# Heads of a gated mixer: one masked step in place of three decay levels, the first turned inverse copied by ScalarE, another order on VectorE

## What is computed

```python
def hgrn2_chunked(q, k, v, log_f):
    b_cum = jnp.cumsum(log_f, axis=3)
    def step(S, inp):
        q_c, k_c, v_c, b_c = inp
        inter = jnp.einsum('bhtk,bhkv->bhtv', q_c * jnp.exp(b_c), S)
        diff = b_c[:, :, :, None, :] - b_c[:, :, None, :, :]
        decay = jnp.exp(jnp.where(causal, diff, -jnp.inf))
        scores = jnp.einsum('bhtk,bhsk,bhtsk->bhts', q_c, k_c, decay)
...
def gated_delta_chunked(q, k, v, beta, g):
...
    A = jnp.where(strict, jnp.einsum('bhntk,bhnsk->bhnts', kb, k) * Lmat, 0.0)
    T = lax.linalg.triangular_solve(eye + A, jnp.broadcast_to(eye, A.shape),
                                    left_side=True, lower=True, unit_diagonal=True)
```

## Time and profile before

| | |
|---|---|
| median of 3 runs | 1363.9 us (1363.88 to 1363.91) |
| the profiled execution, its own time | 1364.0 us |
| its span, first to last instruction | 1362.3 us |
| TensorE busy | 1348.9 us, 99% |
| VectorE busy | 1044.2 us, 77% |
| ScalarE busy | 797.6 us, 59% |
| DMA, mean over the span | 167 GB/s, 227.80 MB |
| granted TensorE clock | 1.000 of 2.4 GHz |

### The profile page before, as it was taken

The page is one execution under the profiler, slowest core; times in us unless marked ns, Lnnn a source line. Parts: engine busy times, 40 slices in busy tenths (PEclk is TensorE's granted clock), DMA queues, the critical chain, the costliest instruction groups (busy, mean ns, idle before and its releaser), DMA issues.

```text
span 1362.3 us, 24396 instructions
## 1 busy us (share of the span) xinstructions
PE 1348.9 (99%) x8590; PEld 1210.5 (89%) x8590; DVE 1044.2 (77%) x1644; ACT 797.6 (59%) x1352; POOL 29.4 (2%) x72
## 2 busy tenths in 40 slices
PE   8999999999999999999999999999999999999998
PEld 8888888989888888888899999999999998988887
DVE  5798888777666686666778898898898877666665
ACT  4445554644334364444668898898898853544444
POOL 6000000000000010000000000000000000000000
PEclk9999999999999999999999999999999999999999
DMA  8565555556555756666564444554543286666661
GB/s 267 153 194 153 149 147 160 190 194 206 185 185 187 226 150 209 186 185 185 155 183 136 132 123 131 135 148 115 149 131 123 88 211 203 173 205 197 191 186 62
DMA packets 291214, 227.80 MB, mean 167 GB/s; under 512 B 10882, under 2 KB 270164, under 8 KB 291156
## 3 DMA queue, kind: packets, MB, share of 16 engines
q1 hardware_dynamic: 291012, 226.75, 56.0%
q10 hardware_dynamic: 144, 0.26, 0.1%
HBM read 225.90 MB, written 1.08 MB: 167 GB/s over the span
## 4 chain that ended last, share of the span: by engine, by line
PE 93%; DVE 3%; ACT 1%; issue 1%; DVEq 1%; ACTq 0%; DMA 0%; POOL 0%; SPq 0%; POOLq 0%
PE M L2119 10%; PE G L2119 9%; PE M L2107 7%; PE M L2108 7%; PE M L2109 7%; PE G L2102 5%; PE G L2104 5%; PE G L2103 5%; PE M L2121 5%; PE G L2121 5%; PE G L2245 2%; PE G L3007 2%; PE M L2830 1%; PE M L2812 1%; PE G L3009 1%; PE G L2109 1%
## 5 line engine op out<-in xcount | busy, mean ns | idle before, releaser
L1241 DVE TENSOR_TENSOR w_lo<-w_raw,w_hi 128x2048 fp32r<-128x2048 f32 (+2 forms) x247 | 478.0, 1941 | 126.4 <-ACT w_hi L655 120.6
L655 ACT ACTIVATE w_hi<-w_raw 128x2048 fp32r<-128x2048 f32 x197 | 375.9, 1909 | 169.5 <-PE M L2121 54.3
L2102 PE MATMUL G<-xa,w_hi 128*128 128x256 f32 x592 | 176.9, 299 | 0.0
L2104 PE MATMUL G<-xa,w_lo 128*128 128x256 f32 x592 | 167.3, 283 | 0.0
L2103 PE MATMUL G<-xa,w_hi 128*128 128x256 f32 x592 | 167.0, 282 | 0.0
L2119 PE MATMUL M<-xa,w_hi 128*128 128x512 f32 x600 | 151.6, 394 | 0.0
L2119 PE MATMUL G<-xa,w_hi 128*128 128x512 f32 x568 | 142.4, 393 | 0.0
L2119 PEld LDWEIGHTS M<-xa,w_hi 128*128 128x128 f32 x600 | 107.8, 189 | 19.8
L2119 PEld LDWEIGHTS G<-xa,w_hi 128*128 128x128 f32 x568 | 104.0, 188 | 21.2 <-issue 1.2
L2107 PE MATMUL M<-w_hi,xb 128*128 128x512 f32 x300 | 117.3, 391 | 0.1
L2108 PE MATMUL M<-w_lo,xb 128*128 128x512 f32 x300 | 117.1, 390 | 0.0
(11 more groups left out here) (461 smaller groups left out, 2545.2 us busy)
## 6 DMA issues: line engine op xcount, KB each, us to landing
w_raw<-in_w_in SPq DMA_DIRECT2D x150, 512.0 KB, 4.7
w_raw<-in_ffn_w_in SPq DMA_DIRECT2D x88, 512.0 KB, 5.0
w_raw<-in_w_ff SPq DMA_DIRECT2D x64, 512.0 KB, 4.1
w_raw<-in_ffn_w_out SPq DMA_DIRECT2D x44, 512.0 KB, 4.9
w_raw<-in_w_in SPq DMA_DIRECT2D x33, 256.0 KB, 3.2
w_raw<-in_w_out SPq DMA_DIRECT2D x16, 512.0 KB, 4.1
w_raw<-in_w_branch_gdn SPq DMA_DIRECT2D x16, 512.0 KB, 5.3
w_raw<-in_w_branch SPq DMA_DIRECT2D x12, 512.0 KB, 4.2
```

Source lines behind the costliest of these rows:

```text
L655: nc.scalar.activation(w_hi[:, slot, :], w_raw[:, slot, :], ACT.Copy).then_inc(hi_ready, 1)
L1241: return v.tensor_tensor(dst, src, hi.bitcast(F32), ALU.subtract)
L2102: mm(out_, w[0], x[0], start=first, stop=False)
L2104: return mm(out_, w[1], x[0], start=False, stop=last_)
```

## The change

Levels 0, 1 and 2 become one step, still called level 0, for groups of four tokens. middle(0) subtracts from hb the value at the second token of each group, and caps the last one's distance from below at -80 (FAR). level_exp(0) makes both exp(-d) and exp(d) for all 256 columns. decayed(0) makes decayed keys and decayed queries in full. level(0) multiplies them in two 128 x 128 matmuls (the second block with its operands exchanged), at the place of level(1). VectorE clears sct with a memset, settles, and scored(0) copies under a group mask. GpSimd builds the two group masks into the free slots lmask 1 and lmask_t 0, with four additions. The counts of the semaphores follow (7 steps a head in place of 8 or 9; step_of).

inv_t(0) and y_copy(0) go: ScalarE writes yc from yi with four copies of 64 partitions, at the end of the head before, ahead of z_copy(1). n21's copy moves to behind level_exp(3). On VectorE inverse(1) comes ahead of both halves of w_low for chunk 1 and scored(0) behind them. In head(0), middle(0) and w_low for the next head's chunk 0 come ahead of the copy of tok. In the loop, middle(0) stands where middle(1) and middle(2) stood.

The diff, cut to its core:

```diff
@@ -624,6 +633,12 @@
 
         for l in range(LEVELS):
             level(l)
+        settle()
+        done(nc.gpsimd.tensor_tensor(lmask[:, 1, :], lmask[:, 1, :], lmask[:, 0, :], ALU.add))
+        done(nc.gpsimd.tensor_tensor(lmask_t[:, 0, :], lmask_t[:, 0, :], lmask_t[:, 1, :], ALU.add))
+        settle()
+        done(nc.gpsimd.tensor_tensor(lmask[:, 1, :], lmask[:, 1, :], ident[:], ALU.add))
+        done(nc.gpsimd.tensor_tensor(lmask_t[:, 0, :], lmask_t[:, 0, :], ident[:], ALU.add))
 
         c = FIRST["ffn1"]
         slot = c % RING
...
@@ -969,8 +984,12 @@
                 ins.then_inc(tap_ready, 1)
 
             def level_exp(l, turn=i):
-                act.wait_ge(dd_ready, l + (turn - 1) * 8)
+                act.wait_ge(dd_ready, step_of(l) + 1 + (turn - 1) * STEPS_H)
                 buf = dd[:, l % 2, :]
+                if l == 0:
+                    nc.scalar.activation(dd[:, 1, :], dd[:, 0, :], ACT.Exp, scale=-1.0)
+                    nc.scalar.activation(dd[:, 0, :], dd[:, 0, :], ACT.Exp).then_inc(lev_exp, 1)
+                    return
                 if l == 8:
                     nc.scalar.activation(buf[:, 0:P], buf[:, 0:P], ACT.Exp, scale=-1.0)
                     nc.scalar.activation(buf[:, P:T], hb[:, P:T], ACT.Exp).then_inc(lev_exp, 1)
@@ -1009,10 +1028,8 @@
             def y_copy(l):
                 if not main:
                     return
-                act.wait_ge(yt_done, l + 1 + (i - 1) * 6)
-                if l == 0:
-                    nc.scalar.activation(yc.rearrange("p i c -> p (i c)"), M[:, 5, 0:T], ACT.Copy).then_inc(yy_ready, 1)
-                elif l < LEVELS - 2:
+                act.wait_ge(yt_done, l + (i - 1) * 5)
+                if l < LEVELS - 2:
                     nc.scalar.activation(halved(yc.rearrange("p i c -> p (i c)"), l, 1), halved(M[:, 5, 0:T], l, 1),
                                          ACT.Copy).then_inc(yy_ready, 1)
                 else:
@@ -1074,7 +1091,6 @@
                 o_hi(1, 0, 2)
             if main:
                 z_copy(1)
-                y_copy(0)
             if not gemm:
                 o_hi(2, 2, 4)
             if main:
@@ -1087,6 +1103,7 @@
                 z_copy(2)
                 y_copy(1)
                 level_exp(3)
+                nc.scalar.activation(n21, nt[:, :, :, HD:P], ACT.Copy)
             if not gemm:
                 split_half(FIRST["yh"] + 2, 0)
             compact(2)
...
@@ -1194,9 +1211,12 @@
                 for side in range(2):
                     ins = nc.scalar.activation(kept(xc, side), quad(x0, side), ACT.Copy)
                 ins.then_inc(xc_ready, 1)
-                level_exp(1, i + 1)
-                level_exp(2, i + 1)
-                nc.scalar.activation(n21, nt[:, :, :, HD:P], ACT.Copy)
+                level_exp(0, i + 1)
+                for side in range(2):
+                    half = slice(HD * side, HD * side + HD)
+                    for e in range(2):
+                        ins = nc.scalar.activation(yc[HD * e:HD * e + HD, :, half], yi[half, :, e, half], ACT.Copy)
+                ins.then_inc(yy_ready, 1)
 
         head(0, True, False)
         with act.Fori(1, GH) as i:
@@ -1787,6 +1807,13 @@
             def middle(l):
                 if l > 2 and not main:
                     return
+                if l == 0:
+                    fours = hb.rearrange("p (n s) -> p n s", s=4)
+                    far = dd[:, 0, :].rearrange("p (n s) -> p n s", s=4)
+                    v.tensor_tensor(far, fours, fours[:, :, 1:2].to_broadcast([P, T // 4, 4]), ALU.subtract)
+                    settle()
+                    v.tensor_scalar(far[:, :, 3:4], far[:, :, 3:4], -FAR, None, ALU.max).then_inc(dd_ready, 1)
+                    return
                 if l == 8:
                     v.tensor_tensor(dd[:, 0, 0:P], hb[:, 0:P], hb[:, P - 1:P].to_broadcast([P, P]), ALU.subtract
                                     ).then_inc(dd_ready, 1)
@@ -1799,7 +1826,11 @@
             def decayed(l):
                 if not main:
                     return
-                dve.wait_ge(lev_exp, l + (i - 1) * 8)
+                dve.wait_ge(lev_exp, step_of(l) + 1 + (i - 1) * STEPS_H)
+                if l == 0:
+                    v.tensor_tensor(kqd[:, 0, :], hk, dd[:, 1, :], ALU.mult)
+                    v.tensor_tensor(kqd[:, 1, :], hq, dd[:, 0, :], ALU.mult).then_inc(wl_ready, 1)
+                    return
                 sz = 1 << (l - 1)
                 if l == 8:
                     v.tensor_tensor(kqd[:, 0, 0:P], hk[:, 0:P], dd[:, 0, 0:P], ALU.mult)
@@ -1813,12 +1844,12 @@
             def scored(l):
                 if not main:
                     return
-                dve.wait_ge(lev_done, l + 1 + (i - 1) * 9)
+                dve.wait_ge(lev_done, step_of(l) + 1 + (i - 1) * STEPS_H)
                 ps = M[:, 2 - 2 * (l % 2), 0:P] if 0 < l < 8 else M[:, 1 if l == 0 else 2 if gemm else 0, 0:T]
-                both_b = [P, 2, P]
                 if l == 0:
-                    v.tensor_tensor(sct[:, 0:T].rearrange("p (i c) -> p i c", i=2), ps.rearrange("p (i c) -> p i c", i=2),
-                                    ident[:].unsqueeze(1).to_broadcast(both_b), ALU.mult).then_inc(sc_used, 1)
+                    dve.sem_inc(waited, 1)
+                    v.copy_predicated(sct[:, 0:T].rearrange("p (i c) -> p i c", i=2), group_masks.bitcast(I32),
+                                      ps.rearrange("p (i c) -> p i c", i=2)).then_inc(sc_used, 1)
                 elif l == 8:
                     v.tensor_copy(sct[:, P:3 * P], ps).then_inc(sc_used, 1)
                 else:
@@ -1871,24 +1902,25 @@
 
             if not gemm:
                 o_low(1, 0, 2)
-            decayed(1)
-            decayed(2)
-            if main and gemm:
-                w_low_half(c0 + 4 + RING - 6, 0, i, 6)
+            decayed(0)
             inverse(1)
+            if main:
+                v.memset(sct[:, 0:T], 0.0)
             if not gemm:
                 o_low(2, 2, 4)
             if main and gemm:
+                w_low_half(c0 + 4 + RING - 6, 0, i, 6)
                 w_low_half(c0 + 4 + RING - 6, 1, i, 6)
+            if main:
+                settle()
             scored(0)
             middle(3)
-            scored(1)
             if main and gemm:
                 w_low_half(c0 + 5 + RING - 6, 0, i, 6)
             inverse(2)
             middle(4)
             decayed(3)
-            scored(2)
+            settle()
             middle(5)
             decayed(4)
             inverse(3)
@@ -2015,8 +2047,8 @@
                 v.scalar_tensor_tensor(out=hk, in0=eh, scalar=lb1[:, ds(i, 1)], in1=hr,
                                        op0=ALU.mult, op1=ALU.mult).then_inc(qk_ready, 1)
                 settle()
-                middle(1)
-                middle(2)
+                if main:
+                    middle(0)
                 v.tensor_tensor(mt, kk[:, 1, :].unsqueeze(1).to_broadcast([P, 2, P]), lt[:, :, P:T], ALU.mult)
                 settle()
                 dve.wait_ge(qk_done, i + 1)
@@ -2024,12 +2056,13 @@
                     ins = v.scalar_tensor_tensor(out=lt[:, e, :], in0=M[:, 3, 0:3 * P], scalar=QSCALE, in1=lt[:, e, :],
                                                  op0=ALU.mult, op1=ALU.mult)
                 ins.then_inc(lt2_ready, 1)
+                if not main:
+                    middle(0)
+                    w_low(c0 + 3 + RING, i, 6)
                 dve.wait_ge(tok_done, i + 1)
                 v.tensor_copy(tok[:, 0, :], G[:, 1, :]).then_inc(evac[1], 1)
                 if main:
                     delta_out_low(i)
-                else:
-                    w_low(c0 + 3 + RING, i, 6)
             settle()
 
         dve.sem_inc(ogl_ready, 1)
...
@@ -2769,15 +2802,11 @@
             def level(l):
                 if not main:
                     return
-                if l == 0:
-                    pe.wait_ge(qk_ready, i)
-                    left, right = hk, hq
-                else:
-                    pe.wait_ge(wl_ready, l + (i - 1) * 8)
-                    if l == 1:
-                        pe.wait_ge(tok_ready, i)
-                    if l > 1:
-                        pe.wait_ge(sc_used, (l if l == 8 and not gemm else l - 1) + (i - 1) * 9)
+                pe.wait_ge(wl_ready, step_of(l) + 1 + (i - 1) * STEPS_H)
+                if l == 3:
+                    pe.wait_ge(tok_ready, i)
+                if l > 0:
+                    pe.wait_ge(sc_used, step_of(l - 1 if l == 8 and not gemm else max(l - 2, 0)) + 1 + (i - 1) * STEPS_H)
                     left = right = kqd[:, l % 2, :]
                 if l == 8 and gemm:
                     mm(M[:, 2, P:T], left[:, 0:P], right[:, P:T], start=True, stop=True)
@@ -2788,10 +2817,9 @@
                     out_ = M[:, 0, P:T] if l == 8 else M[:, 2 - 2 * (l % 2), 0:P]
                     mm(out_, left[:, 0:P], right[:, P:T], start=True, stop=True).then_inc(lev_done, 1)
```

(11 more changed lines are left out.)

15 lines of the change are left out of this document (10 added, 5 removed).

## The result

| | before | after | forecast |
|---|---|---|---|
| median of 6 runs | 1363.8 us | 1369.4 us | 1365.8 (1361.0 to 1368.3) |
| lowest and highest | 1363.2, 1363.9 | 1367.9, 1370.1 | |
| profiled execution, own time | 1364.0 us | 1369.45 us | |
| its span | 1362.3 us | 1367.6 us | |
| granted TensorE clock | 1.000 | 0.998 | |

What follows compares the result with a forecast made beforehand. TensorE's own stream was taken as the bound, with VectorE's chain becoming late after the change; 6 x 0.07 for loop heads, 1.1 for head 1 and 0.4 for head 8 gave +1.9, 1365.8 us, range 1361.0 to 1368.3.

Steps and rivals of the forecast that it cites:

- What TensorE saves: Start of each head: the two turns (0.23) and level 0's old place (0.44) go, saving 0.67 us.
- ScalarE before inv_w(1): ScalarE's exponentials and four copies ahead of z_copy(1) make TensorE wait 0.05 us a head, bounds 0 and 0.4.
- VectorE's chain from inv_w(1) to inv_z(3): VectorE's operations sum to 6.93 us against 6.31 of matmuls, so TensorE waits 0.62 in every loop head.
- step 2: Term of VectorE's chain: inverse(1) to the next operation's start, 0.52 us.
- step 5: Term of VectorE's chain: settle, wait, sem_inc and copy_predicated issue ahead of scored(0), a gap of 0.26 us.
- rival C: The gap between the halves and scored(0) vanishes under the half's end: 1364.0 us, chance 0.12.
- Behind the wait: The first four matmuls after TensorE's wait for inverse(2) take 0.68 instead of 0.61: 0.07 us a loop head.
- Head 1: Quarter 0 waits for the later copy of tok; with the other heads' waits, head 1 loses 1.1 us.
- the 0.69 that the sum had for inverse(2): In head 1, the wait for inverse(2) and slower matmuls behind it, 0.62 + 0.07 us as in other heads.
- Head 8: Last head: ScalarE sets inv_w(1) already and gets more work in front, +0.4 us, bounds 0 and 0.7.
- A: TensorE stays the bound, no wait at inv_z(3), passes of 48.6: 1360.8 us, chance 0.20.
- B: ScalarE's four copies, at 0.39 each, delay z_copy(1) and inv_w(1) by 0.35 more in seven heads: 1368.3 us, chance 0.22.

Runs made afterwards that it cites:

- best_turn: Kernel after with w_low behind tok's copy, memset ahead of inverse(1), chunk 2's half behind middle(5), TensorE's turn restored, n21 moved in head 8 only: 1360.6 us.
- a_mem: Kernel after with only VectorE's memset of sct moved ahead of inverse(1): 1367.7 us.
- a_tok: Kernel after with only head 0's order undone, the copy of tok again ahead of w_low: 1367.9 us.
- a_all: Kernel after with w_low behind tok's copy, memset ahead of inverse(1), chunk 2's half behind middle(5), n21 behind y_copy(2): 1365.3 us.
- a_half: Kernel after with only the w_low half for chunk 2 moved from ahead of inverse(2) to behind middle(5): 1365.2 us.
- a_all_turn: As a_all, but TensorE turns the first inverse again and ScalarE's four copies are gone: 1362.5 us.

## Why the prediction was wrong, step by step

In the loop the mechanism was the one forecast, and two of its terms were too small; in head 1 the drop of the clock was missing from it. The matmuls go, VectorE's chain from inverse(1) to inverse(2) becomes the bound of this stretch, and head 1 waits for the copy of tok. The sign was the forecast's too, but each of the three parts of the sum came out larger: 6 x 0.43 = 2.6 for 0.4, head 1 1.9 for 1.1, head 8 and the rest 0.9 for 0.4.

- **What TensorE saves (0.67 a head): right.** best_turn, which keeps only the 0.44 of level 0, has passes of 48.83, which is 49.27 - 0.44.
- **ScalarE before inv_w(1) (0.05): failed, it is 0.27** in the pass (2.14 against 1.87), and with it 0.22 of the 0.36 that each pass lost beyond the forecast, the largest of the missed terms (1.3 us in six passes). The copies were nearly right in size: 1.26 / 4 = 0.315 for 0.30. z_copy(1) ends at 774.09, which is also when TensorE's own work ends (773.61 and four matmuls at 0.12 from start to start). The step took it that TensorE would go on 0.05 later. It goes on 0.24 later, with 0.25 noted at the weight load, and does so in all six passes of this profile. What this time is made of stays open: in head 8 the same pair, z_copy(1) and inv_w(1), has 0.05 between (the rows above) and before had 0.09. The Trainium skill (ScalarE: Activation LUTs, What ACT_TABLE_LOAD costs) led to an estimated 0.29 for such a copy; the trace has 0.315.
- **VectorE's chain from inv_w(1) to inv_z(3) (6.93): nearly right, 7.04.** Its terms: 0.83 until inverse(1) for 0.76; inverse(1) to the memset 0.74 for 0.52; memset to the halves 0.19 for 0.20; the halves 2.29 with a gap of 0.20 for 2.37 and 0.26; scored(0) 0.54 for 0.55; middle(3) 0.35 for 0.34; the half 1.13 for 1.15; inverse(2) 0.72 for 0.73; to TensorE 0.05. The term that failed is step 2. 0.52 was read from an inverse with a w_low behind it, but this memset begins 0.74 behind the start of the copy_predicated ahead of it, which is 0.75 long. a_mem prices the memset by its absence: the chain is 0.28 shorter, where the sum had 0.20 for it, since without it the halves start earlier but take 0.09 longer. The gap of step 5 is there, at 0.20 for 0.26, so rival C falls: the memset and the halves overlap by 0.08 (775.90 + 0.27 against 776.09), the halves and scored(0), with a drain and a wait between, are 0.20 apart. By the rule of the Trainium skill (VectorE: DVE Perf Modes, Rules for kernel authors), that the pipe empties behind each operation anyway, there would have been none; the measured row decides.
- **Behind the wait (0.07): 0.10.**
- **Head 1 (1.1): failed, 1.9.** The wait itself was right to a tenth (722.30 for 722.41). Missing was that TensorE, idle for 1.83, gets a slower clock afterwards: the working counted the matmuls behind the wait at their old durations. In inv_w(1) it shows as 724.26 for 723.91, and from there to inv_z(2) are 2.98, where a_tok has 1.95. In return the 0.69 that the sum had for inverse(2) in this head doesn't occur: TensorE reaches inv_z(3) (731.68) only when inverse(2) has just ended (731.62). With the chain at 7.04 and no drop the head would have lost an estimated 1.2 (4.16 to inv_w(1), 7.04 to inv_z(3) and 0.10 behind it, against 10.08 before). a_tok gives 1.5 back in the median. The old order had 0.53 idle there and kept its clock. No row of before in the heads had an idle time like 1.83, and that should have been an upward bound of its own.
- **Head 8 (0.4): half.** inv_w(1) is +0.33, as forecast. "n21 moves to where ScalarE waits for VectorE" is true in the loop and false in the last head, where it makes the half of a split and compact(2) 0.31 later; a_all gives just 0.31 back between inv_z(3) and inv_t(2). The other 0.21 of the 0.52 there goes with level_exp(3), which waits 0.61 for VectorE's middle(3) in the kernel after and for nothing before; that this is its cause was not tested. The last 0.12 stand between inv_w(1) and inv_w(2).
- **The rivals.** A (no wait) did not occur, and no run reached its passes of 48.6: with the wait gone a_half has 49.07. That best_turn's 1360.6 lies beside A's 1360.8 is chance, since best_turn saves 0.44 a head instead of 0.67 and doesn't have A's losses in heads 1 and 8. B's mechanism occurred beside the forecast, not in place of it, with 0.22 beyond the forecast a pass instead of 0.35. I had let the two exclude each other; added up they give the range a top above 1368.3. Nor was the top added up from the forecast's own bounds: 0.6 in six heads, 1.1 for head 1 and 0.7 for head 8 are 5.4, or 1369.3, and the bounds of the steps themselves add up to -0.49 and +0.74 a head, not to -0.4 and +0.6. The +0.43 of the loop was inside either. The chance of slower, 0.30, was too low for the same reason, and because what the sum held at zero (the clock behind a long wait, n21 in head 8) could only cost.

What each part costs, taken back alone from the kernel after: the place of chunk 2's half 4.2 us, of w_low in head 0 1.5, of the memset 1.7, ScalarE's copies 1.0. That the four add up to 8.4 for the 8.8 by which best_turn is below is partly chance. The half and the memset shorten one and the same wait, and with it gone (0.83 a pass, 5.0 in six) there is nothing left to gain, so together they bring less than 5.9; ScalarE's copies cost more, 2.8, once that wait is gone (a_all against a_all_turn); and the 1.5, the 1.7 and the 1.0 are each within the spread that the intervals of the totals allow.

Still open: the makeup of the 0.24, the cause of 0.21 and 0.12 in head 8, and what the clock's drop answers to beyond the idle time, since the same idle time brings it in one run and not in another.

## What to carry to other kernels

When matmuls are taken out of a stream that is 99% busy, first write out the chain of the engine that answers between them, with what stands ahead of each answer: here three operations of VectorE (a memset, a half of a w_low, a whole w_low) stood ahead of answers that don't need them, and their places decided whether the change was slower or faster. Costs that were hidden should be added, not set against each other as alternatives, once the cover is gone. An operation has to be priced at every place at which it will stand, the first and last round of the pipeline too, because the neighbours there differ.
